# Two feed-forwards on one core: the down product by seven block products, with VectorE forming the sums and the up tiles going through one bank

## The reference

```python
for l in range(DEPTH):                       # DEPTH = 2
    ...
    h2 = _rms_norm(x, ln2_g[l])
    ff = jnp.square(jax.nn.relu(jnp.einsum('bsd,df->bsf', h2, w_ff1[l])))   # 1024 -> 4096
    x = x + jnp.einsum('bsf,fd->bsd', ff, w_ff2[l])                         # 4096 -> 1024
```

## Time and profile before

| what | value |
|---|---|
| timed runs | 2498.78, 2496.67, 2496.72 us, median 2496.72 |
| span of the profiled execution | 2499.3 us (no other time of its own is given) |
| TensorE busy | 2440.1 us, 98% of the span |
| VectorE, ScalarE, GpSimd busy | 651.3, 418.3 and 53.8 us |
| chain that ended last | 91% on TensorE, 5% on a transfer (moe weights), 2% on VectorE |
| feed-forward of layer 0, and of layer 1 | 317.65 to 539.6 us, and 849.6 to 1070.8 us |

### The profile page before, as it was taken

The page is one execution under the profiler, slowest core; times in us unless marked ns, Lnnn a source line. Parts: engine busy times, 40 slices in busy tenths (PEclk is TensorE's granted clock), DMA queues, the critical chain, the costliest instruction groups (busy, mean ns, idle before and its releaser), DMA issues.

```text
span 2499.3 us, 27928 instructions
## 1 busy us (share of the span) xinstructions
PE 2440.1 (98%) x11210; PEld 1540.3 (62%) x11211; DVE 651.3 (26%) x1441; ACT 418.3 (17%) x1052; POOL 53.8 (2%) x110
## 2 busy tenths in 40 slices
PE   9999999999999999999999999988999989999998
PEld 6666466656565566676777756547996544445444
DVE  0453210011543134455244362101002101011101
ACT  1243010010441132211113112101001101010101
POOL 0000000000000000000000000000000000000000
PEclk9999999999999999999999999998999999999999
DMA  6323344334232688444667458998567999779971
GB/s 263 122 102 126 109 169 168 140 119 157 102 113 106 241 304 312 184 157 169 249 286 303 158 220 362 426 425 368 219 277 300 427 426 426 317 303 425 426 293 80
DMA packets 78971, 617.33 MB, mean 247 GB/s; under 512 B 5984, under 2 KB 6112, under 8 KB 39184
## 3 DMA queue, kind: packets, MB, share of 16 engines
q1 hardware_dynamic: 73920, 558.39, 56.0%
q0 software_dynamic: 4656, 56.47, 5.8%
q10 hardware_dynamic: 288, 0.90, 0.1%
HBM read 614.69 MB, written 1.05 MB: 246 GB/s over the span
## 4 chain that ended last, share of the span: by engine, by line
PE 91%; DMA 5%; DVE 2%; issue 1%; POOL 0%; ACT 0%; SPq 0%; DVEq 0%; POOLq 0%; ACTq 0%
PE G L2160 9%; PE S L2485 8%; PE S L2487 8%; PE G L1883 6%; PE G L1925 5%; DMA big<-in_moe_pack 4%; PE S L2153 4%; PE T L2153 4%; PE G L2501 4%; PE G L2499 4%; PE G L2107 3%; PE S L2371 3%; PE T L2371 3%; PE G L2394 3%; PE S L2553 2%; PE G L2223 2%
## 5 line engine op out<-in xcount | busy, mean ns | idle before, releaser
L2485 PE MATMUL S<-big,hT 128*64 128x256 f32 x2240 | 270.7, 384 | 27.2 <-DMA big<-in_moe_pack 25.6
L2485 PEld LDWEIGHTS S<-big,hT 128*64 128x64 f32 x2240 | 158.4, 137 | 136.6 <-issue 54.3
L2160 PE MATMUL G<-big 128*128 128x512 f32 x512 | 222.2, 592 | 0.0
L1781 DVE TENSOR_TENSOR probs<-S,probs 128x128 f32<-128x128 f32 (+2 forms) x105 | 35.5, 338 | 680.3 <-ACT probs L1100 680.1
L2487 PE MATMUL S<-big,hT 128*128 128x512 f32 x448 | 201.3, 593 | 2.1 <-issue 2.1
L1925 PE MATMUL G<-big,hT 128*128 128x384 f32 x512 | 171.0, 488 | 0.0
L2160 PEld LDWEIGHTS G<-big 128*128 128x128 f32 x512 | 97.2, 190 | 116.0 <-issue 115.3
L1883 PE MATMUL G<-big,hT 128*128 128x372 f32 x512 | 160.8, 476 | 0.4 <-DMA big<-in_proj_pack 0.4
L2487 PEld LDWEIGHTS S<-big,hT 128*128 128x128 f32 x448 | 82.8, 190 | 96.5 <-issue 96.5
L1883 PEld LDWEIGHTS G<-big,hT 128*128 128x128 f32 x512 | 97.0, 190 | 63.4 <-DMA big<-in_proj_pack 1.0
L1925 PEld LDWEIGHTS G<-big,hT 128*128 128x128 f32 x512 | 95.8, 190 | 65.3 <-issue 4.0
(11 more groups left out here) (363 smaller groups left out, 2735.2 us busy)
## 6 DMA issues: line engine op xcount, KB each, us to landing
big<-in_moe_pack SPq DMA_DIRECT2D x112, 2048.0 KB, 15.7
big<-in_moe_pack SPq DMA_DIRECT2D x112, 1024.0 KB, 17.5
big<-in_w_ff SPq DMA_DIRECT2D x32, 2048.0 KB, 8.5
big<-in_ada_pack POOLq DMA_DIRECT2D x24, 2048.0 KB, 14.1
big<-in_ffn_pack SPq DMA_DIRECT2D x11, 3072.0 KB, 14.5
big<-in_gate_pack SPq DMA_DIRECT2D x16, 1536.0 KB, 6.3
big<-in_proj_pack SPq DMA_DIRECT2D x15, 1488.0 KB, 6.2
big<-in_branch_heads SPq DMA_DIRECT2D x6, 2048.0 KB, 7.9
```

The costliest lines, as they stand in the source:

```text
L2160: return mm(G[j][:, :], hid[:, c % 2, f, b * P:(b + 1) * P], w[:, f, half * 512:(half + 1) * 512], start=(c == 0 and f == 0), stop=(c == 7 ...
L2485: ins = mm(S[s % 2][f * FEW:(f + 1) * FEW, 0:SEQ], hTe[:, k, 0:FEW], wt[:, k, f * SEQ:(f + 1) * SEQ], start=(k == 0), stop=(k == KD - 1))
```

## The change

The down product of a chunk is now a 2 by 2 block product: the hidden activations are cut in token halves and hidden halves, the chunk's down weights in hidden halves and column halves, and seven block products (`down_product`, two products of 128x512 each, 14 in place of 16) take the place of the eight. Each of the seven adds up over the chunks in a bank of its own: G0, T1, S1, S0, G3, G1, G2 for products 1 to 7 (`P7`). The products need sums: four of activations (`hidden_sums`: s1 to s4, 128x256 each) and four of weights (`weight_sums`: t1 to t4, 128x1024 each, t3 written over the weights themselves), which VectorE forms after the chunk's squares, once the former chunk's seven products are done with the buffers, and ahead of the modulation's pieces.

With seven banks held, one is left for the up tiles: from chunk 1 on all go through T0 (`up_bank`), and tile f waits for the Relu of the tile before it. TensorE runs chunk c's up tiles with the products of chunk c-1 between them: tile, products 1 and 2, tile, 3 and 5, tile, 7 and 6, tile, 4 (`PRODUCTS`). The last chunk's seven come behind its fourth tile's product 4 of chunk 6, in the order of `LAST_PRODUCTS`. The quarters of `x` are put together from the seven banks at the end of the layer by twelve VectorE operations of 128x512 (a copy, two sums, nine scaled additions) where four stood before. ScalarE's program is as before but for the bank that it reads and, in layer 1's first norm, the order of two sums of squares. In the second block, a semaphore of its own for two VectorE writes of `x` gave way to the step counter.

Line numbers of the new kernel: Relu 1027, square 1548, hidden sums 1555 to 1560, weight sums 1567 to 1572, modulation rows 1256 and 1262, row sums 870, up tiles 2239, seven products 2253.

```diff
-QUARTERS = ((0, 1, 2, 3), (0, 2, 1, 3))
-BY_ROWS = QUARTERS[1]
+BY_ROWS = (0, 2, 1, 3)
+PRODUCTS = (1, 2, 3, 5, 7, 6, 4)
+LAST_PRODUCTS = ((1, 2, 6, 7, 4, 5, 3), (1, 2, 6, 5, 3, 7, 4))
...
+        w_t1 = rot[:, 0:1024].rearrange("p (f n) -> p f n", f=2)
+        w_t2 = arena[:, 2048:3072].rearrange("p (f n) -> p f n", f=2)
+        w_t4 = arena[:, 3072:4096].rearrange("p (f n) -> p f n", f=2)
+        h_sum = rot[:, 1024:2048].rearrange("p (i f s) -> p i f s", i=4, f=2)
+        s1, s2, s3, s4 = (h_sum[:, i] for i in range(4))
+        u2, u3 = o[:, 0, :], o[:, 1, :]
...
+        def summed(l, c, name):
+
+            return sums_ok.at(l, 8 * c + ("s3", "s1", "s2", "s4", "t1", "t3", "t2", "t4").index(name) + 1)
+
+        def up_bank(c, f):
+
+            return (T[0] if c else H4[f])[:, 0:SEQ]
...
-                        act.activation(hid[:, c % 2, f, :], H4[f][:, 0:SEQ], ACT.Relu).then_inc(ff_relu.sem, 1)
+                        act.activation(hid[:, c % 2, f, :], up_bank(c, f), ACT.Relu).then_inc(ff_relu.sem, 1)
                     if l == DEPTH - 1:
...
+                def square(c, f):
+
+                    dve.wait_ge(ff_relu.sem, l * 32 + (c * 4 + f + 1 + 4))
+                    dve.tensor_tensor(hid[:, c % 2, f, :], hid[:, c % 2, f, :], hid[:, c % 2, f, :], ALU.mult).then_inc(ff_ev.sem, 1)
+
+                def hidden_sums(c):
+
+                    h = hid[:, c % 2]
+                    a11, a12, a21, a22 = h[:, 0:2, 0:P], h[:, 2:4, 0:P], h[:, 0:2, P:], h[:, 2:4, P:]
+                    dve.wait_ge(ff_ev.sem, ff_ev.at(l, 4 * c + 4))
+                    dve.tensor_tensor(s3, a11, a21, ALU.subtract).then_inc(sums_ok.sem, 1)
+                    dve.tensor_tensor(s1, a21, a22, ALU.add).then_inc(sums_ok.sem, 1)
+                    dve.wait_ge(sums_ok.sem, summed(l, c, "s1"))
+                    dve.tensor_tensor(s2, s1, a11, ALU.subtract).then_inc(sums_ok.sem, 1)
+                    dve.wait_ge(sums_ok.sem, summed(l, c, "s2"))
+                    dve.tensor_tensor(s4, a12, s2, ALU.subtract).then_inc(sums_ok.sem, 1)
+
+                def weight_sums(c):
+
+                    dve.wait_ge(loaded[(25 + 2 * c) % NSLOT].sem, (l * (L1_CHUNKS // NSLOT) + (25 + 2 * c) // NSLOT + 1) * 16)
+                    w = slot(25 + 2 * c).rearrange("p (f n) -> p f n", n=D)
+                    w11, w12, w21, w22 = w[:, 0:2, 0:512], w[:, 0:2, 512:], w[:, 2:4, 0:512], w[:, 2:4, 512:]
+                    dve.tensor_tensor(w_t1, w12, w11, ALU.subtract).then_inc(sums_ok.sem, 1)
+                    dve.wait_ge(sums_ok.sem, summed(l, c, "t1"))
+                    dve.tensor_tensor(w12, w22, w12, ALU.subtract).then_inc(sums_ok.sem, 1)
+                    dve.tensor_tensor(w_t2, w22, w_t1, ALU.subtract).then_inc(sums_ok.sem, 1)
+                    dve.wait_ge(sums_ok.sem, summed(l, c, "t2"))
+                    dve.tensor_tensor(w_t4, w21, w_t2, ALU.subtract).then_inc(sums_ok.sem, 1)
+
                 for j in range(8):
                     for f in range(4):
-
-                        dve.wait_ge(ff_relu.sem, l * 32 + (j * 4 + f + 1 + 4))
-                        dve.tensor_tensor(hid[:, j % 2, f, :], hid[:, j % 2, f, :], hid[:, j % 2, f, :], ALU.mult).then_inc(ff_ev.sem, 1)
+                        square(j, f)
+                    if j:
+                        dve.wait_ge(used[(23 + 2 * j) % NSLOT].sem, used_at(l, 23 + 2 * j))
+                    hidden_sums(j)
+                    weight_sums(j)
                     if l == DEPTH - 1:
                         for c in ADA_SLOTS[0][j]:
                             ada(0, c)
@@ -1537,20 +1588,56 @@
                 dve.wait_ge(x_new.sem, added(l * 2 + 1))
                 if l == DEPTH - 1:
                     dve.wait_ge(final_in.sem, 16)
-                for i, j in enumerate(QUARTERS[l]):
-                    if i < 3:
-                        dve.wait_ge(ff2_mm.sem, ff2_mm.at(l, i + 1))
+
+                def done(i):
+
+                    if i == LAST_PRODUCTS[l][-1]:
+                        dve.wait_ge(used[39 % NSLOT].sem, used_at(l, 39))
                     else:
-                        dve.wait_ge(used[39 % NSLOT].sem, used_at(l, 39))
-                    add_quarter(j, small[:, 306:308])
-                    if (l, i) == (0, 1):
-                        turned_pair(l * 2 + 2, 1, xn_turned, T[1], hT_dve, gainc[l + 1][0])
-                    if (l, i) == (1, 1):
-                        scale_rows(0)
-                    if (l, i) == (1, 2):
-                        joint_rows(0)
+                        dve.wait_ge(ff2_mm.sem, ff2_mm.at(l, LAST_PRODUCTS[l].index(i) + 1))
+
+                def grow(half, b, src):
+
+                    xs = x[:, b, half * 512:(half + 1) * 512]
+                    return dve.scalar_tensor_tensor(out=xs, in0=src, scalar=small[:, 306 + b:307 + b], in1=xs, op0=ALU.mult, op1=ALU.add)
+
+                done(1)
+                step.did(dve.tensor_copy(u2, P7[1][:, :]))
+                step.do(grow(0, 0, P7[1][:, :]))
+                done(2)
+                grow(0, 0, P7[2][:, :]).then_inc(x_new.sem, 1)
+                done(6)
+                step.do(dve.tensor_tensor(u2, P7[6][:, :], u2, ALU.add))
                 if l == 0:
+                    done(7)
+                    step.did(grow(1, 0, u2))
+                    step.do(dve.tensor_tensor(u3, P7[7][:, :], u2, ALU.add))
+                    step.do(grow(0, 1, u3))
+                    done(4)
+                    grow(0, 1, P7[4][:, :]).then_inc(x_new.sem, 1)
+                    turned_pair(l * 2 + 2, 1, xn_turned, T[1], hT_dve, gainc[l + 1][0])
+                    step.do(grow(1, 1, u3))
+                    done(5)
+                    grow(1, 1, P7[5][:, :]).then_inc(x_new.sem, 1)
+                    step.do(grow(1, 0, P7[5][:, :]))
+                    done(3)
+                    grow(1, 0, P7[3][:, :]).then_inc(x_new.sem, 1)
                     turned_pair(l * 2 + 2, 3, xn_turned, T[1], hT_dve, gainc[l + 1][0])
+                else:
+                    step.do(grow(1, 0, u2))
+                    done(5)
+                    step.do(grow(1, 0, P7[5][:, :]))
+                    done(3)
+                    grow(1, 0, P7[3][:, :]).then_inc(x_new.sem, 1)
+                    scale_rows(0)
+                    done(7)
+                    step.do(dve.tensor_tensor(u3, P7[7][:, :], u2, ALU.add))
+                    step.did(grow(0, 1, u3))
+                    step.do(grow(1, 1, u3))
+                    grow(1, 1, P7[5][:, :]).then_inc(x_new.sem, 1)
+                    joint_rows(0)
+                    done(4)
+                    grow(0, 1, P7[4][:, :]).then_inc(x_new.sem, 1)
...
-                        ins = mm(H4[f][:, 0:SEQ], w[:, k, f * P:(f + 1) * P], hT[:, k, :], start=(k == 0), stop=(k == KD - 1))
+                        ins = mm(up_bank(c, f), w[:, k, f * P:(f + 1) * P], hT[:, k, :], start=(k == 0), stop=(k == KD - 1))
                     return ins
 
-                def down_part(c, f, j):
-
-                    half, b = divmod(j, 2)
-                    w = slot(25 + 2 * c).rearrange("p (k n) -> p k n", k=4)
-                    return mm(G[j][:, :], hid[:, c % 2, f, b * P:(b + 1) * P], w[:, f, half * 512:(half + 1) * 512],
-                              start=(c == 0 and f == 0), stop=(c == 7 and f == 3))
+                def down_product(c, i):
+
+                    h = hid[:, c % 2]
+                    w = slot(25 + 2 * c).rearrange("p (f n) -> p f n", n=D)
+                    left = {1: h[:, 0:2, 0:P], 2: h[:, 2:4, 0:P], 3: s4, 4: h[:, 2:4, P:], 5: s1, 6: s2, 7: s3}[i]
+                    right = {1: w[:, 0:2, 0:512], 2: w[:, 2:4, 0:512], 3: w[:, 2:4, 512:], 4: w_t4, 5: w_t1, 6: w_t2, 7: w[:, 0:2, 512:]}[i]
+                    if i in (1, 2, 4):
+                        pe.wait_ge(ff_ev.sem, ff_ev.at(l, 4 * c + (2 if i == 1 else 4)))
+                    if i > 2:
+                        pe.wait_ge(sums_ok.sem, summed(l, c, {3: "s4", 4: "t4", 5: "t1", 6: "t2", 7: "t3"}[i]))
+                    for f in range(2):
+                        ins = mm(P7[i][:, :], left[:, f, :], right[:, f, :], start=(c == 0 and f == 0), stop=(c == 7 and f == 1))
+                    return ins
...
                     for f in range(4):
-                        pe.wait_ge(ff_relu.sem, ff_relu.at(l, 4 * c + f + 1))
+                        pe.wait_ge(ff_relu.sem, ff_relu.at(l, 4 * c + f + (4 if c else 1)))
                         up_part(c, f, KH if c == 0 else 0, KD).then_inc((ff_mm if f < 3 else used[2 * c % NSLOT]).sem, 1)
-                    for d in (c,) if c < 6 else (6,) if c == 7 else ():
-                        weights(l, 25 + 2 * d)
-                        for f in range(4):
-                            pe.wait_ge(ff_ev.sem, ff_ev.at(l, 4 * d + f + 1))
-                            for j in range(4):
-                                ins = down_part(d, f, j)
-                        ins.then_inc(used[(2 * d + 1) % NSLOT].sem, 1)
```

(14 more changed lines are left out.)

20 lines of the change are left out of this document (11 added, 9 removed).

## The result

| | before | changed kernel |
|---|---|---|
| median of the runs | 2497.38 us (4 runs, 2496.67 to 2498.78) | 2539.93 us (4 runs, 2535.77 to 2541.16) |
| ratio | | 1.0167, interval 1.0152 to 1.0181 |
| span of the profiled execution | 2499.3 us | 2537.0 us |
| time of the profiled execution | 1.85 us above the span, if as after: about 2501.1 | 2538.85 us |

The changed kernel is 42.5 us slower by the medians; 34.2 were forecast. Between the two profiled executions the difference is 37.7 us, since that of the kernel before was itself some 4 us above its median.

The account below looks back on a forecast made before the run. TensorE, busy 98% of the span at nearly full clock, was taken as the bound. -27.5 + 1.3 + 4.1 + 42.9 + 9.6 + 3.8 = +34.2 us on 2496.7 gave 2530.9 us, range 2520 to 2543.

Parts of the forecast that it names:

- Parts 1 to 3: Both layers' feed-forwards: fewer products -27.5 us, one bank for up tiles +1.3 us, VectorE's sums behind the last chunk +4.1 us.
- Part 4: Layer 1: TensorE waits for ScalarE, held by row sums, after chunks 1, 2, 4 and 5: +42.9 us.
- Part 5: TensorE at half clock behind each of layer 1's four waits, 2.4 us each: +9.6 us, bounds 0 and 20.
- Part 6: End of layer 1: VectorE finishes its additions and joint rows after TensorE's last product: +3.8 us, bounds 2 and 6.
- ScalarE is not in the way: Faster rival, layer 1: next chunk's first Relu not behind the row sums; -18.3 us remain, 2478.4 us; chance 4%.
- The clock that does not come back: Slower rival, layer 1: waiting chunks run their products at half clock, +103 in place of 9.6, 2624 us; chance 2%.
- part 2: One bank for up tiles: Relu hidden except at the start of chunk 1, both layers +1.3 us; bank-rotation advice implied 34 us.
- The weights were never late: Rival on feed-forward weight loads: late loads cost chunks a few us each, +5 to +15, 2536 to 2546 us; chance 5%.

Follow-up runs that it names:

- e1_rows_first: Changed kernel with layer 1's modulation pieces put ahead of the eight sums on VectorE: 2513.78 us, ratio 1.0063.
- e4_sums_old_order: Kernel before, with its 16 products and TensorE order, plus VectorE's eight sums per chunk, unused by products: 2498.94 us, ratio 1.0001.
- e2_spread: Changed kernel with layer 1's eight row sums spread on ScalarE behind the next chunk's first three Relus: 2487.78 us, again 2486.54 us.
- e5_dose: Changed kernel with weight sum t1 formed seven times in chunks 1, 2, 4 and 5 of layer 1: 2570.29 us, ratio 1.0282.
- e6_end: Kernel with spread row sums, VectorE's operations at the end of layer 1 reordered: 2488.32 us, ratio 0.9950.

## Why the prediction was right, and by how much it was off

The direction, the mechanism and its place were right, and 2539.9 lies within 2520 to 2543. By the steps:

- **Parts 1 to 3, layer 0**: forecast -13.7 + 0.6 + 2.0 = -11.1 us, measured -10.8. The waits are 0.56 and 1.87 us, and a pair of products is 1.72 us from start to start, as counted.
- **Part 4, the row sums**: forecast 11.7 + 3 x 10.4 = 42.9 us of waiting, measured 11.47 + 3 x 10.21 = 42.1. None after chunks 3 and 6. The split in 3.0 for the interleaving and 7.4 for the sums was measured as 2.86 and 7.35 (e1_rows_first). That it needs both is shown by e4_sums_old_order, that it is in ScalarE's order by e2_spread, and its slope by e5_dose.
- **Part 5, the clock**: forecast 9.6 us behind the four waits, measured 7.0 in one trace of the changed kernel and 9.5 in the other. In the first trace the stretch at half is shorter than the 4.7 us of the earlier trace rows: 0.70 over 5.2 us is some 3.1 us at half, all within one tile. In the second the four losses average 2.4 us, the forecast's own figure. The working had the grant fall during the wait, as it did here; that a wait of 3 us costs nearly as much it did not say (e1_rows_first).
- **Part 6, the end**: forecast 3.8 us, measured 3.22 of waiting. The mis-sized term is what comes behind it: the transposes and the four records of 128x512 after it run partly at the lower clock, 4.34 us from 1102.23 to 1106.57 where 2.59 stood before. I had given that wait no clock loss, +1.75. The path was also not the one counted: I added up VectorE's operations alone, and the last to end is the chain over ScalarE and GpSimd, by 0.20 us in the changed kernel and 1.06 us in e6_end; the kernel before had such a wait too, 0.29 us. Two of GpSimd's operations in it (lines 783 and 785) take 0.45 and 0.58 us where the kernel before has 0.20 each; why was not tried.
- **Layer 1 as a whole**: forecast -13.7 + 0.6 + 2.0 + 42.9 + 9.6 + 3.8 = +45.2, measured +44.1 and +46.6 in the two traces.
- **The sum against the median**: the two feed-forwards gave +33.3 in the first trace (44.1 - 10.8) for the forecast +34.2. The medians differ by 42.5. 4.4 us of that are in the last column of the table, in code that the change hardly touches. 3.7 come from the base: I read the profiled execution of before as 2.6 us above its median by its span, while a time is a span and 1.85 us more, and I carried a difference worked out from that trace over to the median. 1.1 is the changed kernel's profiled execution lying below its own median. The range had no term for any of these; it held the result only because the bound on the clock was wide, and that much is luck.

Of the rivals: that ScalarE is not in the way was wrong for the changed kernel. With the order changed so that it is not, e2_spread gave 2487.8 and 2486.5, and I had put 2478.4 for that case. The two feed-forwards gave -16.5 for the -18.3, which is the clock at the end of layer 1 again (1.75), and the last stretch of the program gave back another 4.0 and 2.3 us in those traces; by the medians of their sets they are 11.4 and 12.8 us faster than before. The clock that does not come back did not happen: it was full in the products right behind each slow tile. But the argument against it, that waits of 1.6 us in the expert stage leave the clock full, does not reach far: waits of 2.86 to 4.12 us in e1_rows_first lowered it each time. For the advice to rotate banks, which part 2 takes from the Trainium skill ("Perfetto Trace Analysis", Optimizing Tensor Performance, Matmuls), the trace shows both halves: of 28 tiles per layer that go through T0, one waits in layer 0 (0.56 us) and five in layer 1, so products in other banks in between do for a Relu of 0.4 us; but where ScalarE's next work was 9 us long the single bank carried it to TensorE whole. The weights were never late.

## What to carry to other kernels

When tiles share one bank, ask not how long its reader takes but what is written ahead of it on the reader's engine, and what that waits for in turn: here three engines in a row, VectorE's sums, ScalarE's row sums, TensorE's tile. A change that saves products on the full engine and adds work to idle ones is decided by such orders; moving 32 row sums among the Relus turned +1.7% into -0.6%. Take the cheap reordering of the helper's list into the change before judging the idea.
